# Key copies, query copies and centring around the norm of a two-block float32 model

## The reference

```
x = layer_norm(ALPHA * x + h, ln_g[i, 0], ln_b[i, 0])              # h: the layer's attention
x = layer_norm(ALPHA * x + memory_cross_attention(x, mem, ...), ln_g[i, 1], ln_b[i, 1])
x = layer_norm(ALPHA * x + conv_glu(x, ...), ln_g[i, 2], ln_b[i, 2])

def memory_cross_attention(x, mem, w_q, w_kv, w_o):
    q = x @ w_q;  k, v = split(mem @ w_kv)        # 4 heads of 256
    s = q k^T / 16;  p = softmax(s);  return (p v) @ w_o
```

## Time and profile before

| | us |
|---|---|
| median of 3 runs | 2804.84 (2803.47 to 2805.12) |
| span of the profiled execution | 2793.4 |
| TensorE busy in it | 2665.3 (95%) |
| VectorE, ScalarE, POOL busy | 1260.4, 1202.4, 986.0 |

### The profile page before, as it was taken

How to read it: one execution, slowest core, us unless ns; L and a number is a source line. 1 busy time by engine, 2 the same in 40 slices (tenths; PEclk the granted TensorE clock), 3 DMA queues, 4 the chain that set the end, 5 groups by cost and what they waited for, 6 DMA issues and landing times.

```text
span 2793.4 us, 36140 instructions
## 1 busy us (share of the span) xinstructions
PE 2665.3 (95%) x13862; PEld 2144.1 (77%) x13862; DVE 1260.4 (45%) x2335; ACT 1202.4 (43%) x1762; POOL 986.0 (35%) x437
## 2 busy tenths in 40 slices
PE   7998999999999999999988989999979999989998
PEld 5774787788887888888867767888858877767776
DVE  2555615443235122223247164532349235257997
ACT  3555433523235243434344334232353355346775
POOL 3220543444445423323315224444432345432000
PEclk9999999999999999999999999999988999999999
DMA  4111321333233522222213222333223412239997
GB/s 156 61 46 46 116 89 67 106 98 105 91 87 118 159 76 76 61 76 62 75 61 106 76 61 75 92 105 91 91 64 106 149 64 68 69 104 330 397 397 297
DMA packets 321737, 319.33 MB, mean 114 GB/s; under 512 B 16538, under 2 KB 278059, under 8 KB 320980
## 3 DMA queue, kind: packets, MB, share of 16 engines
q1 hardware_dynamic: 319284, 309.36, 33.9%
q0 software_dynamic: 2288, 7.88, 0.7%
q10 hardware_dynamic: 16, 0.03, 0.0%
HBM read 308.27 MB, written 20.53 MB: 118 GB/s over the span
## 4 chain that ended last, share of the span: by engine, by line
issue 47%; PE 29%; POOL 16%; DMA 3%; DVE 2%; ACT 1%; SPq 1%; POOLq 0%; ACTq 0%; DVEq 0%
POOL wl L721 12%; PE ps L2101 9%; PE ps L2103 8%; PE ps L2102 8%; POOL wl L718 4%; DMA e_raw<-in_w_up 2%; DVE e_wl L1888 1%; PE ps L2097 1%; SPq L659 1%; PE ps L2437 1%; DMA sorted_x<-e_tok,p_row 0%; PE ps L2515 0%; ACT e_wh L1358 0%; PE ps L2534 0%; DMA e_raw<-in_w_down 0%
## 5 line engine op out<-in xcount | busy, mean ns | idle before, releaser
L718 POOL TENSOR_TENSOR wl<-raw,wh 128x1024 fp32r<-128x1024 f32 (+1 forms) x191 | 453.2, 2373 | 1526.6 <-ACT wh L785 1526.5
L2101 PE MATMUL ps<-xh,wh 128*128 128x512 f32 x1680 | 680.7, 405 | 50.6 <-POOL wl L721 17.2
L2102 PE MATMUL ps<-xh,wl 128*128 128x512 f32 x1680 | 664.2, 395 | 0.0
L2103 PE MATMUL ps<-xl,wh 128*128 128x512 f32 x1680 | 663.9, 395 | 0.0
L721 POOL TENSOR_TENSOR wl<-raw,wh 128x1024 fp32r<-128x1024 f32 (+1 forms) x191 | 478.5, 2505 | 0.0
L785 ACT ACTIVATE wh<-raw 128x1024 fp32r<-128x1024 f32 (+1 forms) x191 | 198.7, 1040 | 565.3 <-PE ps L2103 561.5
L2101 PEld LDWEIGHTS ps<-xh,wh 128*128 128x128 f32 x1680 | 321.3, 191 | 148.4 <-issue 48.4
L2103 PEld LDWEIGHTS ps<-xl,wh 128*128 128x128 f32 x1680 | 321.1, 191 | 69.9
L2102 PEld LDWEIGHTS ps<-xh,wl 128*128 128x128 f32 x1680 | 322.0, 192 | 62.9
L2101 PE MATMUL ps<-ah,wh 128*128 128x512 f32 x608 | 239.7, 394 | 5.8 <-DVE X L1584 2.9
L2103 PE MATMUL ps<-al,wh 128*128 128x512 f32 x608 | 236.8, 389 | 0.0
(11 more groups left out here) (368 smaller groups left out, 4050.9 us busy)
## 6 DMA issues: line engine op xcount, KB each, us to landing
raw<-in_ffn_w_in SPq DMA_DIRECT2D x88, 512.0 KB
raw<-in_dil_w_qkv SPq DMA_DIRECT2D x72, 512.0 KB
e_raw<-in_w_gate SPq DMA_DIRECT2D x56, 512.0 KB, 12.1
e_raw<-in_w_up SPq DMA_DIRECT2D x56, 512.0 KB, 12.8
e_raw<-in_w_down SPq DMA_DIRECT2D x56, 512.0 KB, 11.7
raw<-in_w_in SPq DMA_DIRECT2D x42, 512.0 KB
raw<-in_xatt_w_kv SPq DMA_DIRECT2D x32, 512.0 KB
raw<-in_ffn_w_out SPq DMA_DIRECT2D x32, 512.0 KB
```

The source lines that it names most:

```text
L718: pool.tensor_tensor(wl[:, s, 0:4, 0:n], raw[:, s, 0:4, 0:n], wh[:, s, 0:4, 0:n].bitcast(F32), ALU.subtract)
L2101: pe.matmul(dst, stat_h, mov_h, start=first, stop=False)
L2102: pe.matmul(dst, stat_l, mov_h, start=False, stop=False)
L2103: return pe.matmul(dst, stat_h, mov_l, start=False, stop=last)
```

## The change

Three edits. In the key units both halves of a unit go into one PSUM bank, side by side, and units take banks 0 and 1 in turn. TensorE waits for the unit two back (`emptied`), or for the last unit ahead of the keys. ScalarE copies a unit out with one instruction of 128 by 512 when both halves are done, and converts weights behind it; the copy raises `drained` by two. In the query units the conversion moves behind both copies. In the six layer norms VectorE centres two chunks ahead of the wait for Exp in place of four, and chunks 2 and 3 in the loop.

```diff
@@ ScalarE, memory_unit(k) @@
                     u = Lin(u0 + k)
-                    done(u, 0)
-                    act.activation(x_k[:, 2 * k], bank(0)[:, 0:M], ACT.Copy).then_inc(drained[slot_of(u)], 1)
                     done(u, 1)
+                    act.activation(x_k[:, 2 * k:2 * k + 2], bank(k % 2).rearrange("p (j m) -> p j m", j=2), ACT.Copy
+                                   ).then_inc(drained[slot_of(u)], 2)
                     high(u + 2)
-                    act.activation(x_k[:, 2 * k + 1], bank(1)[:, 0:M], ACT.Copy).then_inc(drained[slot_of(u)], 1)
@@ ScalarE, queries(u, k) @@
                     for j in range(2):
                         done(u, j)
-                        if j == 1:
-                            high(u + 2)
                         act.activation(x_q[:, (k * 2 + j).at(), :], ps[:, j:j + 1],
                                        ACT.Copy).then_inc(drained[slot_of(u)], 1)
+                    high(u + 2)
@@ VectorE, norm @@
-                    for c in range(4):
+                    for c in range(2):
                         centre(c)
                 dve.wait_ge(ln_act, on_act)
...
-                            if c >= 4:
+                            if c >= 2:
                                 centre(c)
@@ TensorE @@
+            def memory_keys(u, k):
+
+                s = begin(u)
+                if k < 2:
+                    free(u + -k, k)
+                else:
+                    emptied(pe, u + -2)
+                for j in range(2):
+                    cols = slice(j * P, (j + 1) * P)
+                    for kc in range(KC):
+                        mm = triple(ps[:, k % 2, j * M:(j + 1) * M], wh[:, s, kc, cols], wl[:, s, kc, cols],
+                                    mh[:, kc], ml[:, kc], kc == 0, kc == KC - 1)
+                    mm.then_inc(chunk_done, 1)
...
                 for k in range(4):
-                    columns(Lin(U_MEM[layer] + k), mh, ml, width=M)
+                    memory_keys(Lin(U_MEM[layer] + k), k)
```

## The result

| | median | runs |
|---|---|---|
| before | 2804.49 us | 4 (2803.47 to 2805.12) |
| after | 2783.41 us | 4 (2782.13 to 2787.93) |

The ratio is 0.9927, with an interval of 0.9914 to 0.9939: the change takes 0.73% (21.1 us) off, where the prediction had 5.5 us. Between the two profiled executions the difference is smaller, 2793.4 - 2780.3 = 13.1 us. Why the two differ is part of what follows.

What follows compares the result with a forecast made beforehand. The prediction took TensorE, busy 95% of the span, as the bound. Key units -2.0, query copies -3.8 and norms +0.3 gave -5.5 us: 2793.4 - 5.5 + 11.4 around the span = 2799.3 us, range 2793.5 to 2803.5.

Steps and rivals of the forecast that it cites:

- Key units: Memory key units beside each layer's first norm: one copy frees both banks, the second stop goes, -2.0 us over both layers.
- Query copies: Last query unit: its copy moves ahead of two conversions, so scores start 1.91 us earlier per layer, -3.8 us in all.
- Norms 0 to 4: Centring edit: zero in norms 0 and 3, +0.5 us in norm 1, +0.6 in norm 2, +0.1 in norm 4.
- Norm 5: Centring edit where ScalarE paces the norm: the chain starts 0.97 us earlier and stays so, -0.9 us.
- Norm 1: Centring edit where a conversion holds ScalarE: early products buy nothing, the last low part comes 0.5 us later, +0.5 us.
- R3: Rival: later stages do not wait for the copies, the score chain absorbs the cuts; only 2.0 and 0.3 remain, 2803.1 us; chance 0.08.
- R4: Rival: VectorE paces all six norms' chunk loops, nothing hides the centrings, +8.5 in place of +0.3, 2807.5 us; chance 0.05.
- the term for the clock: TensorE's clock ahead of the queries and the scores: nothing taken, 3.4 us kept either way for each place.
- The prediction's own sign of being wrong: Wrong if norm 1's chunk 7 low part comes no later, scores don't move 1.9, or clock rows change in several places.
- R1: Rival: the low-clock stretch at layer 0's queries does not come, forecast less 3.4 us, 2795.9 us; chance 0.25.
- R2: Rival: the low-clock stretch comes in layer 1 as well, forecast plus 3.4 us, 2802.7 us; chance 0.12.
- the unbroken gap ahead of the queries: Two stops ahead of the queries (1.24 and 1.14 us) become one of 2.6 us; by the skill's rule this speaks against the change.

Runs made afterwards that it cites:

- e5_all: The kernel after, all three edits, run once more on another chip: ratio 0.9925 to the kernel before, -21.3 us.
- e2_banks: The kernel before with only the key unit edit (two banks in turn, one copy of 512 columns): ratio 0.9983, -4.3 us.
- e10_no_centre: The kernel after without the centring edit, so key units and query copies alone: ratio 0.9956 to the kernel before, -12.8 us.
- e3_queries: The kernel before with only the query copies moved ahead of the conversion: ratio 0.9976, -7.2 us.
- e8_others: The kernel before with the centring edit in the five norms other than norm 5: ratio 0.9999, -0.7 us.
- e1_same: The kernel before, unchanged, run and profiled once more: ratio 1.0002, -0.1 us; its profiled span is 2798.4 us.
- e7_norm5: The kernel before with the centring edit in norm 5 alone: ratio 0.9964, -9.4 us.
- e6_slip: The kernel after with two idle copies on ScalarE ahead of Ln of norm 6: ratio 0.9949 to the kernel before, -15.1 us.
- e9_before_slip: The kernel before with six idle copies on ScalarE, 2.5 us, ahead of Ln of norm 6: ratio 0.9982, -4.5 us.

## Why the prediction was wrong

**The mechanical steps held.** Key units: 1.0 us a layer was forecast, -1.0 shows in the column of the queries in `e5_all`, `e2_banks` and `e10_no_centre` (-1.0, -1.0, -1.1). Query copies: 1.91 a layer, 390.68 - 388.88 = 1.80 in `e3_queries` with an entry 0.2 later, so 2.0. Norms 0 to 4: +1.2 forecast together; `e8_others` has +0.4 from its entry (+2.6) to behind norm 5 (+3.0), and a ratio of 0.9999, so they cost no more than forecast and perhaps less. Norm 5: -0.9 forecast, -0.98 in the timeline. Norm 1 +0.5 forecast, +0.53. The rivals that put the cause into these steps, R3 (absorbed) and R4 (VectorE paces), are refuted by the same rows.

**The step that failed** is the term for the clock, "I take nothing for it, and keep 3.4 either way for each place". In `e5_all` against `e1_same` the last product comes 18.8 us earlier, 18.6 less its early entry; 5.5 are the steps, and 13.1 are left. The time at a granted clock of 0.50, counted over the whole span, is 117.1 us in `e1_same` and 88.3 in `e5_all`. 28.8 us less at half speed do the work of at most 14.4, which is the size of what is left; at most, because TensorE also idles in some of them. The prediction's own sign of being wrong, clock rows that change in more than one place, is met: the start of layer 0's queries, the feed-forward's start and the second block. Three things were wrong in the term:

- *Places.* I looked at two places in each layer. The clock was low for 110.2 us of the profiled execution, 62.4 of it behind product 10350, where the change has no edit, and I priced norm 5's shift at itself. It is worth 9.4 us (`e7_norm5`). In the trace 7.1 us arise between products 10350 and 12096, where the time at 0.50 is 30.7 us for 48.8 in `e1_same`; 3.1 are lost again by the last product.
- *One execution.* The profile of before was a short one: it runs 5 us ahead of `e1_same`, all of it gained by norm 4, with no low stretch behind its scores. I read "the same stops left it at 1.00" as a property of the stops. The 11.4 us "around the span" were mostly this: in every other execution 1.7 to 2.6 us lie around it. It was a sign in plain sight that the profiled execution was not a typical one. An ordinary execution like `e1_same` would have shown the 2.75 ahead of the scores followed by a low stretch in both layers, worth 1.3 to 1.7 us each.
- *Sign.* R1 took one low stretch out of layer 0 (0.25), R2 put one more in (0.12). What R1 said of that place came true (1.00 at 341.60), but its price of 3.4 us was one place's. I weighed them one place at a time. The traces here have 14 to 22 low stretches, an edit that shifts everything behind it can change many of them, and the spread of the sum is wider than 3.4 either way.

The prediction cited the Trainium skill (TensorE: Matmul & The Clock Gate, HAM oscillation) for gaps being what decides, and argued from it that the unbroken gap ahead of the queries speaks against the change. The runs show that the length of such a gap does not settle it here: the stop of 2.64 us at 341.51 in the kernel after is followed by a clock of 1.00, and the stop of 2.65 at 340.52 in `e6_slip`, the same program up to there, by this:

```profile
341.60:345.00 3.40, 3.40 (x10) 0.50 0.50 173
```

What stays open: why a given place is followed by a low stretch at one instant and not at another. The instant matters, as `e6_slip` and `e9_before_slip` show, and in the second block its distance to the clock's last rise tells the two cases apart; a rule that holds for other places I have not found. The clock effect of the key and query parts (7.7 us in `e10_no_centre`) is read off one trace of each kernel, and not all of them add up: `e2_banks` has 10 us more at 0.50 than `e1_same` in a trace 0.2 us shorter. The traces compared in the table also come from three chips.

## What to carry to other kernels

Where TensorE is busy 95% of the time, price a step twice: once by the waits that it removes, and once by the low-clock stretches behind every stop that it shortens and every place that it shifts, over the whole program and not only where the edit is. A stop cut from 2.75 to 0.78 us was worth 1.3 to 1.7 more than the 1.9 cut, in each layer of `e3_queries`; a shift of a microsecond ahead of the second block moved the median by 6 to 9 us, one way (`e7_norm5`) and the other (`e6_slip`). The second price can't be read from one trace; give it a range as wide as that. Test a gain that the timelines don't explain with a pure delay at the same place: if idle work makes the kernel faster, the gain belongs to the instant and not to the edit.

## What the runs showed of the hardware

- Idle work can make a program faster: 2.5 us of copies ahead of norm 6 made the kernel before 0.18% faster (0.9973 to 0.9991), and 0.85 us made the kernel after 6.3 us slower (the ratio to before rose from 0.9925 to 0.9949).
- The time at half clock is 88 to 127 us in traces of kernels that differ by a few instructions. In `e5_all` against `e1_same` it accounts for more of the difference (up to 14.4 us) than the instructions do (5.5); `e2_banks` is an exception.
- Low stretches follow short stops in some executions: 2.75 us ahead of the scores, and even 2.06 us (`q_n`). They also come with no stop, in the midst of 32 products of one column (`e6_slip`, 2184.8). In `e6_slip` these start 79.4 us after the clock's last rise; in `e5_all` they start 80.1 us after it, and no low stretch comes.
- Two executions of one unchanged program can differ by 5 us in span (2793.4 and 2798.4), and most of it goes with the clock: 110.2 against 117.1 us at 0.50, the work of up to 3.5, and TensorE busy 2665.3 against 2670.8.
